# Regrouping the hidden tiles of a SwiGLU block on one Trainium2 core: 3, 6, 6 and 7 tiles in place of 4, 6, 6 and 6

## The reference

```python
x = x + rmsnorm(merged @ w_out, g_mix_post)
h = rmsnorm(x, g_ffn_pre)
f = (silu(h @ w_ffn_gate) * (h @ w_ffn_up)) @ w_ffn_down      # 1024 -> 2816 -> 1024
x = x + rmsnorm(f, g_ffn_post)
x = x + (p @ w_ple_proj) * sigmoid(x @ w_ple_gate)
```

## Time and profile before

| | |
|---|---|
| median of three runs | 976.92 us |
| the profiled execution itself | 976.66 us |
| its span (first to last instruction) | 974.9 us |
| TensorE matmul (PE) busy | 960.3 us, 99% |
| VectorE (DVE) busy | 626.3 us, 64% |
| ScalarE (ACT) busy | 477.0 us, 49% |
| GpSimd (POOL) busy | 156.1 us, 16% |
| DMA | 118.11 MB, mean 121 GB/s |
| granted TensorE clock | 1.0 over the span |

### The profile page before, as it was taken

The page is one execution under the profiler, slowest core; times in us unless marked ns, Lnnn a source line. Parts: engine busy times, 40 slices in busy tenths (PEclk is TensorE's granted clock), DMA queues, the critical chain, the costliest instruction groups (busy, mean ns, idle before and its releaser), DMA issues.

```text
span 974.9 us, 19206 instructions
## 1 busy us (share of the span) xinstructions
PE 960.3 (99%) x7191; PEld 941.3 (97%) x7191; DVE 626.3 (64%) x1273; ACT 477.0 (49%) x913; POOL 156.1 (16%) x222
## 2 busy tenths in 40 slices
PE   8999999999999999999999999999999999999898
PEld 8999999999999999999999999999999999999898
DVE  6554776767665633435458854788878886756772
ACT  5333534444343522223455556776677776753352
POOL 2122212122100000010003001222222222231000
PEclk9999999999999999999999999999999999999999
DMA  8534211222212232246604446666887588777211
GB/s 217 150 113 135 81 52 55 72 76 66 69 56 67 76 97 77 78 128 180 190 3 123 179 130 142 153 154 143 178 187 157 122 189 179 152 189 247 87 50 49
DMA packets 178025, 118.11 MB, mean 121 GB/s; under 512 B 16224, under 2 KB 167168, under 8 KB 177680
## 3 DMA queue, kind: packets, MB, share of 16 engines
q1 hardware_dynamic: 160192, 79.19, 28.6%
q0 software_dynamic: 15856, 36.07, 17.1%
q10 hardware_dynamic: 1888, 1.64, 0.6%
HBM read 86.79 MB, written 10.75 MB: 100 GB/s over the span
## 4 chain that ended last, share of the span: by engine, by line
PE 69%; issue 17%; POOL 5%; DVE 4%; DMA 2%; ACT 2%; POOLq 0%; SPq 0%; DVEq 0%; ACTq 0%
PE acc L794 37%; PE acc L1071 6%; PE acc L1072 6%; PE acc L1073 6%; POOL wlo L2764 5%; PE small L1071 2%; PE small L1072 2%; PE small L1073 2%; DMA raw<-in_w_ple_gate 1%; PE small L940 1%; PE small L986 1%; PE small L957 1%; PE small L990 1%; PE small L949 1%; PE small L988 1%
## 5 line engine op out<-in xcount | busy, mean ns | idle before, releaser
L794 PE MATMUL acc<-xh,whi 128*128 128x288 f32 x720 | 158.7, 302 | 0.6 <-DVE xl L1855 0.4
L1279 ACT ACTIVATE whi<-raw 128x1024 fp32r<-128x1024 f32 (+1 forms) x60 | 60.0, 1001 | 197.4 <-PE acc L794 196.0
L794 PE MATMUL acc<-xl,whi 128*128 128x288 f32 x720 | 153.4, 294 | 0.0
L794 PE MATMUL acc<-xh,wlo 128*128 128x288 f32 x720 | 153.4, 294 | 0.0
L794 PEld LDWEIGHTS acc<-xh,whi 128*128 128x128 f32 x720 | 114.0, 188 | 6.3 <-issue 4.7
L794 PEld LDWEIGHTS acc<-xh,wlo 128*128 128x128 f32 x720 | 115.0, 188 | 0.0
L794 PEld LDWEIGHTS acc<-xl,whi 128*128 128x128 f32 x720 | 114.9, 188 | 0.0
L1071 PE MATMUL acc<-yh,whi 128*128 128x288 f32 x380 | 112.8, 297 | 0.1
L1073 PE MATMUL acc<-yh,wlo 128*128 128x288 f32 x380 | 112.0, 295 | 0.0
L2764 POOL DMA_DIRECT2D wlo<-raw x80 | 69.0, 863 | 251.5 <-ACT wlo L1507 246.8
L1838 DVE TENSOR_TENSOR wlo<-raw,whi 128x1024 fp32r<-128x1024 f32 (+1 forms) x62 | 71.8, 1157 | 44.3 <-ACT whi L1279 43.4
(11 more groups left out here) (383 smaller groups left out, 2450.0 us busy)
## 6 DMA issues: line engine op xcount, KB each, us to landing
raw<-in_w_in SPq DMA_DIRECT2D x91, 256.0 KB, 3.2
wlo<-raw POOLq DMA_DIRECT2D x56, 256.0 KB, 3.8
raw<-in_w_ffn_gate SPq DMA_DIRECT2D x44, 256.0 KB, 3.5
raw<-in_w_ffn_up SPq DMA_DIRECT2D x44, 256.0 KB, 3.6
raw<-in_w_ffn_down SPq DMA_DIRECT2D x48, 192.0 KB, 3.1
res<-x_scratch POOLq DMA_DIRECT2D x16, 288.0 KB, 4.4
wlo<-raw POOLq DMA_DIRECT2D x24, 192.0 KB, 3.7
raw<-in_w_branch_ret SPq DMA_DIRECT2D x16, 256.0 KB, 3.1
```

The costliest lines, as they stand in the source:

```text
L794: ins = nc.tensor.matmul(acc[:, a, hf, 0:HALF], w[:, s, at:at + P], x(k)[:, hf * HALF:(hf + 1) * HALF], start=first and n == 0 and m == 0, ...
L1279: nc.scalar.activation(whi[:, s, 0:n], raw[:, s, 0:n], ACT.Copy).then_inc(hi_ready, 1)
```

## The change

`GROUPS` becomes 3, 6, 6, 7. The three plain tiles form group 0 alone, so its down projection follows the plain tiles at once, before the first seven-product tile; the row-block sums `th`/`tl` are formed beside it. Every product tile is now in group 1, 2 or 3. The last group has seven tiles. The weight of product (3, PA0) takes its low part by the accumulating DMA. The sums of f no longer have a buffer of their own (`f01`): they are all made in place in `f3`, in another order, and `f_high` and three of the four high parts of the sums move behind the copy-out of the next pair's PA0. PS1 of the columns waits only for the lower tiles' sum.

```diff
-GROUPS = (range(0, 4), range(4, 10), range(10, 16), range(16, 22))
+GROUPS = (range(0, 3), range(3, 9), range(9, 15), range(15, 22))
@@ by_dma
-    return t in BY_DMA and (i, t) != (PLAIN, PA0)
+    return t in BY_DMA
@@ PE, sums_wait
+                elif t == PS1:
+                    pe.wait_ge(tf_lo, 4 * LOWER * SUMMED.index(g) + LOWER)
                 else:
-                    pe.wait_ge(tf_lo, 3 * LOWER * SUMMED.index(g) + 3 * (LOWER - 1) + {PS1: 1, PS2: 1, PS3: 2, PB1: 3}[t])
+                    pe.wait_ge(tf_lo, 4 * LOWER * (SUMMED.index(g) + 1) - 3 + {PS2: 1, PS3: 2, PB1: 3}[t])
@@ ACT, behind the plain tiles
-            t_high(0)
-            t_high(1)
             gate_silu(1, 1)
             f_half(1, 1)
-            t_high(2)
-            t_high(3)
+            hi(("down", 0))
+            gate_silu(2, 0)
+            hi(("down", 1))
+            f_half(2, 0)
+            gate_silu(2, 1)
+            hi(("down", 2))
+            f_half(2, 1)
+            hi(("down", 3))
...
@@ ACT, product_out
                 if t == PA0 and before is not None and not is_columns(before):
-                    if g in SUMMED:
-                        f_sums_high(before, (1, 2))
-                    else:
-                        f_high(before)
+                    f_high(before)
+                    f_sums_high(before, (0, 2, 3))
...
-                if t == PB1 and g in SUMMED and not is_columns(i):
-                    f_sums_high(i, (0,))
-                    f_high(i)
+                if t == PB1 and not is_columns(i):
+                    f_sums_high(i, (1,))
@@ ACT, down of group 0 (DVE: t_low(c), lo)
                         if c < 4:
+                            t_high(c)
                             hi(("down", c0 + c + 4))
@@ DVE, product_out (f_sum(i, 1) stands in f_out)
                 elif t == PB1:
                     f_out(i)
...
-                        f_sums(i, True)
-                        f_sums_low(i, 0)
-                        f_low(i)
+                    f_sum(i, 0)
+                    f_sum(i, 2)
+                    f_sums_low(i, 1)
+                if t == PA0 and before is not None and not is_columns(before):
+                    f_sum(before, 3)
+                    f_low(before)
                 if after is not None:
                     product_operand(after, t)
...
                 if t == PA0 and before is not None and not is_columns(before):
-                    if g in SUMMED:
-                        f_sums_low(before, 1)
-                        f_sums_low(before, 2)
-                    else:
-                        f_low(before)
+                    for m in (0, 2, 3):
+                        f_sums_low(before, m)
@@ DVE, the new f_sum: lower tiles m == 0, upper tiles m == 1, 2, 3
+                if m == 0:
+                    ins = nc.vector.tensor_tensor(f3[:, j, :], ta[:, cols(0)], ta[:, cols(1)], ALU.subtract)
+                elif m == 1:
+                    ins = nc.vector.tensor_tensor(f3[:, j, :], f3[:, j, :], ta[:, cols(1)], ALU.add)
+                elif m == 2:
+                    ins = nc.vector.tensor_tensor(f2[:, j, :], ta[:, cols(1)], f2[:, j, :], ALU.subtract)
+                else:
+                    dve.wait_ge(tf_lo, 4 * LOWER * SUMMED.index(g) + LOWER + 3 * j + 1)
+                    ins = nc.vector.tensor_tensor(f3[:, j, :], f3[:, j, :], ta[:, cols(0)], ALU.subtract)
```

More of the change, by code:

```diff
@@ L1669, in f_sums_high @@
                 g = group_of(i)
-                n = i - GROUPS[g][0] - LOWER
-                if g not in SUMMED or n < 0:
+                n = i - GROUPS[g][0]
+                if g not in SUMMED:
                     return
-                made = 4 * LOWER * SUMMED.index(g) + LOWER + 3 * n
+                made = 4 * LOWER * SUMMED.index(g)
                 for m in parts:
[L1675 to L1678, removed]
+                    if (n < LOWER) != (m == 0):
+                        continue
+                    j = n % LOWER
+                    act.wait_ge(tf_sum, made + (n + 1 if m == 0 else LOWER + 3 * j + m))
+                    dst, src = ((f01_h[:, 0, j, :], f3[:, j, :]), (f01_h[:, 1, j, :], f3[:, j, :]),
+                                (f2_h[:, j, :], f2[:, j, :]), (f3_h[:, j, :], f3[:, j, :]))[m]
+                    nc.scalar.activation(dst, src, ACT.Copy, scale=-1.0 if m == 1 else 1.0).then_inc(tf_hi, 1)
             def product_out(i, t, before, after):
@@ L1728, in _ @@
                 c0 = KD * g
-                if g not in SUMMED:
-                    f_high(pairs_of(g)[-1])
+                if c0 == DL:
+                    f_high(FT - 1)
                 if g == 0:
@@ L2329, in _ @@
             f_half_low(0, 1, 2)
-            t_low(0)
-            t_low(1)
             f_half(1, 1, 3)
             f_half_low(1, 1, 3)
+            t_sum(0)
+            lo(("down", 0))
+            t_sum(1)
+            f_half(2, 0, 4)
+            lo(("down", 1))
+            f_half(2, 1, 5)
+            f_half_low(2, 0, 4)
+            f_half_low(2, 1, 5)
+            t_sum(2)
+            lo(("down", 2))
+            t_sum(3)
+            lo(("down", 3))
             def sum_of(i, t):
@@ L2394, in f_sums_low @@
                 g = group_of(i)
-                n = i - GROUPS[g][0] - LOWER
-                if g not in SUMMED or n < 0:
+                n = i - GROUPS[g][0]
+                if g not in SUMMED or (n < LOWER) != (m == 0):
                     return
[L2398 to L2402, removed]
+                made = 4 * LOWER * SUMMED.index(g)
@@ new lines, in f_sums_low @@
+                j = n % LOWER
+                dve.wait_ge(tf_hi, made + (n + 1 if m == 0 else LOWER + 3 * j + m))
+                if m == 1:
+                    nc.vector.scalar_tensor_tensor(f01_l[:, 1, j, :], f3[:, j, :], -1.0, f01_h[:, 1, j, :].bitcast(F32),
+                                                   ALU.mult, ALU.subtract).then_inc(tf_lo, 1)
+                    return
+                dst, src, high = ((f01_l[:, 0, j, :], f3[:, j, :], f01_h[:, 0, j, :]), None,
+                                  (f2_l[:, j, :], f2[:, j, :], f2_h[:, j, :]),
+                                  (f3_l[:, j, :], f3[:, j, :], f3_h[:, j, :]))[m]
@@ L2403, in f_sums_low, with f_sum @@
                 nc.vector.tensor_tensor(dst, src, high.bitcast(F32), ALU.subtract).then_inc(tf_lo, 1)
-            def f_sums(i, late):
+            def f_sum(i, m):
                 g = group_of(i)
                 n = i - GROUPS[g][0]
-                if g not in SUMMED:
+                if g not in SUMMED or (n < LOWER) != (m == 0):
                     return
[L2412 to L2425, removed]
-                                               ALU.subtract).then_inc(tf_sum, 1)
-                nc.vector.tensor_tensor(f2[:, n, :], ta[:, cols(1)], f2[:, n, :], ALU.subtract).then_inc(tf_sum, 1)
-                dve.wait_ge(tf_sum, made + 1)
@@ L2484, in product_out @@
                     f_out(i)
-                    if g in SUMMED:
-                        p4 = ("prod", i, PB1)
-                        dve.wait_ge(bank_read[BANK[p4]], TURN[p4] + 1)
-                        f_sums(i, True)
-                        f_sums_low(i, 0)
-                        f_low(i)
-                if i == PLAIN and t == PS2:
-                    f_half_low(2, 0, 4)
-                    f_half_low(2, 1, 5)
+                    p4 = ("prod", i, PB1)
+                    dve.wait_ge(bank_read[BANK[p4]], TURN[p4] + 1)
+                    f_sum(i, 0)
[4 more added lines that the diff above has]
+                    f_low(before)
                 if after is not None:
@@ L2521, in _ @@
                         product_out(i, t, preceding(g, i), following(g, i))
-                if g not in SUMMED:
-                    f_low(pairs_of(g)[-1])
+                if KD * g == DL:
+                    f_low(FT - 1)
                 if g == 0:
```

32 lines of the change are left out of this document (7 added, 25 removed).

## The result

The changed kernel takes 971.35 us (median of four, 970.49 to 973.23) against 977.62 us (976.76 to 978.38) on the same chip: a ratio of 0.9939, 95% interval 0.992 to 0.9957, that is 6.0 us less (4.2 to 7.8). (The 976.92 us ahead is the median of three of before's runs; the fourth took 978.33 us and makes it 977.62.) The forecast was 969.6 us, with a range of 968.0 to 973.0 over all cases: the median lies in it, and 0.35 us above the range that the forecast gave its own case (968.6 to 971.0). The profiled execution took 970.49 us, 6.2 less than before, where the sum said 7.3.

A forecast was written before the change was run, and what follows sets the result against it. PE's matmuls and its standstills were taken to bound the kernel. Terms -1.15 - 0.24 + 0.2 - 3.1 - 2.1 - 0.95 = -7.3 us on 976.66 gave 969.35, median 969.6 us; own range 968.6 to 971.0, all cases 968.0 to 973.0.

The forecast's parts named there:

- list of signs of being wrong: PE waits on `kept` or `wd` (group 0's down, upper tiles), `wlo<-raw` ((3, PA0), second pair), or `sqacc` above 0.5 us.
- Tile 3, PS2: PE's gap at tile 3, where PS2 waits for PA0's copy-out, goes: -1.15 us, bounds -1.15 and 0.
- Start of group 0: Group 0's down: the old 0.24 us gap waiting for f is replaced by one of 0.2 us, bounds 0 and 0.5.
- Columns: First column pairs of groups 1 and 2: PS1's wait goes, PB1 about 0.4 us late each; together -3.1, bounds -3.9 and 0.
- the rule that was weighed there: Skill page says waiting on a DVE result costs nothing extra; the sum would be 0.4 us lower; forecast followed the rows instead.
- Product tiles: Groups 1 and 2: PS2's copy-out, behind ACT's moved high parts, is in time by 0.65 us, so no cost.
- Tail: Last down and first gate units: column-sums-of-squares gap goes, -2.1 (bounds -2.1, -1.5); gate gap goes, -0.95 (bounds -1.05, -0.5).
- The DMA of (3, PA0): Added DMA lands at 5.7, at most 7.5 us, against PA0's need at 7.16: no wait, bound 0.4 us.
- nothing comes back: Rival: all gaps go, with only 0.2 us left at group 0's start: 968.6 us; chance 0.14.
- the columns give all back: Rival: ACT and DVE have the same work in the first pair, so the columns gain nothing: 972.7 us; chance 0.18.
- the tail's: Rival: gate weights' load lands late regardless, so the sums-of-squares and gate-unit gaps stay: 972.7 us; chance 0.07.
- the two slower ones: Rivals: waits only move, 976.9 us, chance 0.05; ACT's queue delays PS2's copy-out in upper tiles, 979.5 us, chance 0.03.

The follow-up runs named there:

- groups_only: The new groups (3, 6, 6, 7) and new start, with the old sums of f and old columns' wait: 973.29 us (0.9957 of before).
- sums_only: The old groups (4, 6, 6, 6) and old start, with the new sums of f and new columns' wait: 975.74 us (0.9981 of before).
- Experiment 7: Changed kernel with DVE making the next column pair's second weight sum and its low part before the output additions: 971.54 us (0.9933 of before).
- experiments 4 and 5: Changed kernel with tile 4's raw weight loads held until the (3, PA0) DMA landed: both held 972.36 us, only the second 969.79 us.
- experiment 6: Changed kernel with row-block sums t_sum(2) and t_sum(3) moved earlier on DVE, directly behind t_sum(1): 972.05 us (0.9935 of before).
- sum_first: The kernel of Experiment 7: changed kernel with the next pair's second weight sum ahead of the output additions in the columns; 971.54 us.
- after_again: The changed kernel profiled a second time, nothing edited: 972.57 us (969.83 to 975.8, five executions).
- sum_first_again: sum_first profiled a second time, nothing edited: 970.74 us (970.2 to 971.28, two executions).
- early_sums: The kernel of experiment 6: changed kernel with t_sum(2) and t_sum(3) earlier on DVE; 972.05 us (0.9935 of before).

## Why the prediction was right

Its mechanism holds step by step, and one term was mis-sized: the added DMA, put at nothing, cost 1.1 and 1.5 us in the changed kernel's two profiles. A wait on `wlo<-raw` at (3, PA0) stood in its own list of signs of being wrong, and that sign came; the other signs did not.

- **Tile 3, PS2** (-1.15): gone, no distance above 0.2 there. groups_only has it gone as well, sums_only has it still: it is the place of group 0's down that does it.
- **Start of group 0** (-0.24, +0.2): 0.28 at 562.94, a cost of 0.25.
- **Columns** (-3.9, +0.8): the wait on the low part is gone, and at PB1 of the first pair 0.44 and 0.43 stand, each 0.38 with the refill, for the 0.4 of the ledger. Experiment 7 shows the cause that the ledger named. PS2, PA1, PS3 and the next pair's PA0, three of them with 0.1 to 0.3 us left in the ledger, have no gap. In the profiles the columns' term is right to 0.1 us; the 1.9 us of sums_only's median do not bear it out. As to the rule that was weighed there: DVE's row `ta` at 649.27 is followed by `y_full` at 649.76, 0.49 later, and that by a row which needs nothing of it at 650.13, 0.37 later. The rows agree with the earlier trace rows, and the give-back was that of the rows. So the wait costs 0.12 us here, where the Trainium skill's page "VectorE: DVE Perf Modes" has in its section "The DRAIN you can't avoid" that "the semaphore costs nothing extra here". The prediction left out that the same section adds "A next op that is not held starts earlier", and with that sentence the rows agree.

```profile
649.27 0.45 DVE L2442 SCALAR_TENSOR_TENSOR ta<-acc,tb 128x288 f32<-128x288 f32 x1
649.76 0.46 DVE L2418 TENSOR_TENSOR y_full<-ta,y_full 128x288 f32<-128x288 f32 x1
650.13 0.45 DVE L2397 SCALAR_TENSOR_TENSOR f_l<-f,f_h 128x288 fp32r<-128x288 f32 x1
```

- **Product tiles** (0): no gap in the upper tiles of either group.
- **Tail** (-2.1, -0.95): both gone. E, the end of the fourth column of the last down, is 884.11 - 0.20 = 883.91, the last addition to `sqacc` ends at 898.07, E + 14.2 as forecast, and PE comes at 898.21, E + 14.3: a margin of 0.14 us. No gap is left at the first gate units. By the distances of starts the two gaps had cost 2.41 - 0.13 = 2.3 and 1.13 - 0.13 + 0.10 = 1.1 us, 0.3 more together than the sum had for them (for the first it took the bare wait, without what its own rule adds).

```profile
884.11 0.46 DVE L2526 TENSOR_TENSOR wd<-small,wd 128x288 f32<-128x288 f32 x1 [1.32 <-PE small L1072]
...
897.61 0.46 DVE L2534 TENSOR_TENSOR sqacc<-sqacc,sq_out 128x288 f32<-128x288 f32 x1 [0.51 <-ACT sq_out L1750]
```

- **The DMA of (3, PA0)** (0, bound 0.4): mis-sized. It cost 1.15 - 0.13 + 0.10 = 1.1 us in one profile and 1.5 in another. Two things were off. The start is 2.3 us behind the column's end (573.35) and not 1.94, since ACT's first row-block part waits for DVE's `t_sum(3)`, which the ledger of ACT had left out. And the landing took 5.8 and 6.2 us and not the median of 3.8, nor the longest of 5.6: both are over many places of the kernel, and here two loads of 256 KB are asked for 0.5 and 0.05 us before it. By experiments 4 and 5 the landing is the larger part and would do alone: with 3.5 or 3.6 us PE did not wait. The start alone would not: in experiment 6 it was 1.95 behind the column's end, as in the ledger, and PE did not wait because the landing took 5.2 as well.

With the forecast's terms and these 1.1 us the profiled execution comes to 970.45; it took 970.49. That this is so close is luck: 0.2 more each at (15, PA0) and ahead of the plain tiles stand against 0.3 less in the tail. The median is 0.9 above that execution, where the prediction added 0.26, the offset of its three runs of before. By four runs before's own median, 977.62, is 1.0 above its profiled execution, so nothing of the changed kernel is needed to explain the offset. What can make its executions differ the second profile shows: landings at (9, PA0) and (15, PA0), and the clock behind them. Of the rivals, "nothing comes back" fails at PB1 and (3, PA0), "the columns give all back" at PB1 with 0.8 of 3.9, and the tail's and the two slower ones showed none of their waits.

What stays open: why sums_only's executions spread over 4 us, and why its gain is 1.9 us by the median where its profile shows the 3.1. It has the same kind of DMA at the first product behind the columns, but only its fastest execution has a trace, with 0.32 us between starts there. The granted clocks on record account for a part: six of its eleven executions have a mean clock of 0.997 or 0.998 and average 976.3 us, the five at 1.0 average 974.9. Of before's 17 beside them, the six at 1.0 average 977.2, which makes 2.3 us among executions at 1.0. Open too is what makes the landing at (15, PA0) differ between executions of one kernel, and when the clock falls.

## What to carry to other kernels

When waits go, work out who is next to be late, product by product; done from rows, that came out within 0.2 us at every place but one. A median landing is no bound for a DMA on the path: look at what else is asked for in the same microsecond at just that place, and where the slack over the median is under some 2 us (an estimate: the landings here ran up to 3.6 over it) let an engine with time to spare make the operand. Where the executions of one kernel differ by several us, profile it twice before explaining a difference between two kernels.

## What the runs showed of the hardware

- Accumulating DMAs of the same 256 KB landed 3.2 (before) to 7.4 us (sum_first) after their start. At (3, PA0), with a weight load asked for in the same microsecond, it took 5.8, 6.2, 6.1, 6.2, 5.3 and 5.2 us (after, after_again, sum_first, sum_first_again, groups_only, early_sums); with that load held, 3.5 and 3.6.
- At (15, PA0) it varied for one and the same kernel, 4.9 and 6.9 us in two executions of the changed kernel, 7.4 and 4.9 in two of sum_first.
- Distances between PE's starts of 2.61 us (after_again) and 2.16 us (early_sums) were followed by a granted clock of 0.50, the 1.2 GHz level, for some 3.4 us, at once in the one and 1.2 us after PE went on in the other. That cost 1.5 us each time on top of the wait. Distances of 3.15 us (sum_first), 2.41, 2.01 and 2.00 us (before) were not.
- A DVE operation of 128x288 starts 0.37 us after the one before it, and 0.48 to 0.49 when it waits for that one's result (before and after).
